# Two edits late in a two-block transformer kernel: where the second half of the odd attention's output is split, and where a norm's scale column is made

## The reference, cut to what matters

```python
def second_block(x, c, ctx, c_ctx, mod_w, mod_b, ...):
    for l in range(DEPTH):
        sh_a, sc_a, g_a, sh_f, sc_f, g_f = [m[:, None, :] for m in adaln(c, mod_w[l], mod_b[l])]
        ...
        hx = modulate(rms_norm_2(x, norm_mix_g[l]), sh_a, sc_a)
        ...
            y_x, y_c = odd_mixer(hx, hc, need_ctx, od_w_in[e], na_q_g[e], na_k_g[e], na_rpb[e])
        x = x + g_a * (y_x @ w_out[l])
        x = x + g_f * swiglu(modulate(rms_norm_2(x, norm_ffn_g[l]), sh_f, sc_f), ffn_w_in[l], ffn_w_out[l])
```

## Time and profile before

| | us |
|---|---|
| median of three runs | 2492.61 (2489.43 to 2493.49) |
| span of the profiled execution | 2492.5 |
| TensorE busy | 2455.0 (98%) |
| VectorE busy | 1663.2 (67%) |
| ScalarE busy | 1284.4 (52%) |
| GpSimd busy | 225.6 (9%) |

### The profile page before, as it was taken

One profiled execution on the slowest core, in us unless ns is written; L12 is line 12 of the kernel. 1 busy time (PEld: TensorE's weight loads), 2 busy tenths in 40 slices (PEclk: granted clock), 3 DMA queues, 4 the chain that ended last, 5 costly groups with the idle time before them and its releaser, 6 DMA issues.

```text
span 2492.5 us, 40595 instructions
## 1 busy us (share of the span) xinstructions
PE 2455.0 (98%) x16401; PEld 2145.3 (86%) x16401; DVE 1663.2 (67%) x2448; ACT 1284.4 (52%) x1858; POOL 225.6 (9%) x306
## 2 busy tenths in 40 slices
PE   8999999999999999999999999999999999999999
PEld 8998977889989988877898988888899898766998
DVE  5556786775566566776776668786666656776555
ACT  4444645444444446454564555655555445565443
POOL 1000000111002000000111201210000101211000
PEclk9999999999999999999999999999999999999999
DMA  8755565858658655556766546663456667735654
GB/s 285 243 181 179 145 189 158 287 176 299 199 177 275 189 159 165 173 167 227 234 218 183 187 137 212 193 209 120 133 177 197 190 183 203 219 120 177 195 186 144
DMA packets 239370, 479.14 MB, mean 192 GB/s; under 512 B 17584, under 2 KB 38328, under 8 KB 239120
## 3 DMA queue, kind: packets, MB, share of 16 engines
q1 hardware_dynamic: 215664, 397.07, 50.8%
q0 software_dynamic: 23520, 79.49, 9.9%
HBM read 475.33 MB, written 6.92 MB: 193 GB/s over the span
## 4 chain that ended last, share of the span: by engine, by line
PE 87%; DVE 6%; ACT 3%; DMA 2%; issue 2%; POOL 0%; ACTq 0%; SPq 0%; DVEq 0%; POOLq 0%
PE bank L213 84%; PE bank L216 3%; DVE wlo L156 1%; ACT whi L200 1%; DMA raw<-in_od_w_in 1%; DVE bank L161 1%; DVE xl L156 1%; DMA tbias<-t_rows 0%; ACT bank L200 0%; DMA raw<-in_w_mix_out 0%; ACT sps L200 0%; ACT po L200 0%; ACT lb L200 0%; DVE st L176 0%; POOL rs L148 0%
## 5 line engine op out<-in xcount | busy, mean ns | idle before, releaser
L156 DVE TENSOR_TENSOR wlo<-raw,whi 128x1024 fp32r<-128x1024 f32 (+3 forms) x786 | 914.8, 1171 | 616.4 <-ACT whi L200 614.8
L200 ACT ACTIVATE whi<-raw 128x1024 fp32r<-128x1024 f32 (+3 forms) x786 | 794.1, 1018 | 700.4 <-PE bank L213 646.7
L213 PE MATMUL bank<-xh,whi 128*128 128x256 f32 x2208 | 626.1, 284 | 4.2 <-DVE xl L156 3.1
L213 PE MATMUL bank<-xl,whi 128*128 128x256 f32 x2208 | 620.7, 281 | 0.0
L213 PE MATMUL bank<-xh,wlo 128*128 128x256 f32 x2208 | 620.7, 281 | 0.0
L213 PEld LDWEIGHTS bank<-xh,whi 128*128 128x128 f32 x2208 | 417.2, 189 | 15.7 <-issue 7.9
L213 PEld LDWEIGHTS bank<-xl,whi 128*128 128x128 f32 x2208 | 417.3, 189 | 0.6
L213 PEld LDWEIGHTS bank<-xh,wlo 128*128 128x128 f32 x2208 | 417.3, 189 | 0.0
L213 PE MATMUL bank<-whi,xh 128*128 128x512 f32 (+2 forms) x632 | 253.1, 401 | 8.3 <-DVE xl L156 3.9
L213 PE MATMUL bank<-wlo,xh 128*128 128x512 f32 (+2 forms) x632 | 245.6, 389 | 0.0
L213 PE MATMUL bank<-whi,xl 128*128 128x512 f32 (+2 forms) x632 | 245.5, 388 | 0.0
(11 more groups left out here) (455 smaller groups left out, 3763.0 us busy)
## 6 DMA issues: line engine op xcount, KB each, us to landing
raw<-in_ffn_w_in SPq DMA_DIRECT2D x280, 512.0 KB, 4.5
raw<-in_ffn_w_out SPq DMA_DIRECT2D x154, 512.0 KB, 4.5
raw<-in_w_mix_in SPq DMA_DIRECT2D x112, 512.0 KB, 3.6
store<-in_mod_w POOLq DMA_DIRECT2D x46, 512.0 KB, 7.8
raw<-in_od_w_in SPq DMA_DIRECT2D x40, 512.0 KB, 4.9
raw<-in_ffn_w_in SPq DMA_DIRECT2D x56, 256.0 KB, 2.8
stow<-in_mod_w POOLq DMA_DIRECT2D x28, 512.0 KB, 4.7
raw<-in_w_branch SPq DMA_DIRECT2D x24, 512.0 KB, 4.0
```

Source lines behind the costliest of these rows:

```text
L156: return self.passed(out, self.e and self.e.tensor_tensor(out, a, b, op))
L200: return self.made(us, self.e and self.e.activation(out, a, f, **k))
L213: return self.made(n, self.e and self.e.matmul(out, lhs, rhs, **k))
```

## The change

Two edits. In `prenorm`, the scale column is taken before the norm waits for the powers, if `co.modulated` already has what it needs; else at the old place. In `rows`, the attention job is wrapped in `attended`, which after the attention's last step splits the second half itself, into the same tiles `co.xt.hi` and `co.xt.lo`, with the same four operations that `halves` had; `second_half` is a new record of these tiles with marks of its own. The call of `halves` for the second half is gone, and the projection reads `second_half`.

```diff
@@ prenorm
         a[t] = co.po.tensor_tensor(st.rs[:, t, 1:2], st.rs[:, t, 0:1], minus_half(co, st.rs[:, t, 0:1]), ALU.pow).then_inc(co.s_po)
+    gain = mod_gain(co, l, f) if co.modulated >= for_norm(l, f) else None
     yield Need(a)
...
-    yield from modulated(co, for_norm(l, f))
-    gain = mod_gain(co, l, f)
+    if gain is None:
+        yield from modulated(co, for_norm(l, f))
+        gain = mod_gain(co, l, f)
@@ rows
-    heads = spawn(co, od.attend(co.Y, pr, at_, co.smo, co.mxo, at(92, "osel", [8, 512]), co.pn.tile[:, 512:1024], counts(co), done))
+    second_half = Turned(co.xt.hi, co.xt.lo)
+
+    def attended():
+        yield from od.attend(co.Y, pr, at_, co.smo, co.mxo, at(92, "osel", [8, 512]), co.pn.tile[:, 512:1024], counts(co), done)
+        y, second_half.dep = co.Y.tile[:, :, :].rearrange("p t d -> p (t d)").rearrange("p (k n) -> p k n", k=8), []
+        for k in (4, 6):
+            co.ac.wait_ge(tuple(done[1]), second_half.free)
+            a = co.ac.activation(second_half.hi[:, k:k + 2, :], y[:, k:k + 2, :], ACT.Copy).then_inc(co.s_ac)
+            co.dv.wait_ge(a)
+            second_half.dep.append(co.dv.tensor_tensor(second_half.lo[:, k:k + 2, :], y[:, k:k + 2, :], second_half.hi[:, k:k + 2, :].bitcast(F32), ALU.subtract).then_inc(co.s_dv))
+
+    heads = spawn(co, attended())
...
-    free = pe_mark(co)
+    free = second_half.free = pe_mark(co)
...
     while not heads.over:
         yield 0
-    co.xt.free = free
-    yield from halves(co, co.Y, 4, 8, tuple(done[1]), co.xt)
-    yield from out_proj(co, 1, 4, 8, co.xt, gate.make, True)
+    co.Y.free = second_half.dep[1]
+    yield from out_proj(co, 1, 4, 8, second_half, gate.make, True)
+    co.xt.free = pe_mark(co)
```

## The result

The changed kernel takes 2505.81 us (median; 2503.21 to 2507.33) where the kernel before takes 2492.61: a ratio of 1.0052, with a 95% interval of 1.0040 to 1.0063. It is 13 us slower, outside the range that was given, and not the 1.6 us faster that was forecast. Its profiled execution has a span of 2502.4 us, and the run that it belongs to is timed at 2504.39. TensorE does the same work: 2457.6 us busy with as many instructions as in the earlier trace rows.

The account below looks back on a forecast made before the run. TensorE was taken as the bound, busy 2455.0 of 2492.5 us. Terms -3.81 (A), +1.15 (B) and +1.2 (two feed-forward tiles) sum to -1.46, taken as -1.5: 2491.0 us, chance 0.52; range 2487.5 to 2496.0.

Parts of the forecast that it names:

- the term for the six earlier norms: At the six norms before the last, taking the scale early was put at 0, bounds 0 to -0.5 us.
- Rival 2: A readiness test on modelled times flips and rearranges jobs: 3.4 us either way, 2487.6 to 2494.4; chance 0.20.
- B: Around the last norm, up to the feed-forward's first product: TensorE 1.15 us later in the old clock.
- A: Start of the second output projection: its second half starts at 2276.08, not 2279.89, 3.81 us earlier.
- The two tiles pushed on from A: Two modulation tiles of the last but one block aren't done at A but in the last norm's first wait.
- the columns behind the multiplications at the last norm: At the last norm, `mc` follows the multiplications and the scale keeps its old place; ScalarE 0.2 us later from this.
- four loads ahead of the powers: At B, GpSimd issues four loads, not two, before the powers for the norm's roots, making them 0.7 us later.
- The two tiles in the feed-forward: Two modulation tiles stay over and go in the feed-forward's stream, costing 1.2 us.
- Rival 1: Last norm's block is ready, so the scale is taken during the powers: -2.95 us in all, 2489.5; chance 0.12.
- Rival 3: TensorE waits at the last norm and feed-forward for tiles not landed: +2.7 us, 2495.2; chance 0.12.
- Rival 4: The split isn't earlier in effect and the tiles stay at A: 2492.5 us; chance 0.04.
- The row against the early scale: A scale operation took 0.48 us beside GpSimd's ten loads, 0.17 elsewhere; each moved scale might cost up to 0.3 more.

Follow-up runs that it names:

- experiment 2: Kernel before with only the scale column made earlier, the split left in its old place: 2504.40 us, 1.0049.
- experiment 3: Kernel before with the scale column early in the engines' queues only, the plan modelling it at the old place: 2490.44 us, 0.9995.
- experiment 7: Whole change on the engines, but the plan given only the split, with the scale column modelled at its old place: 2490.76 us, 0.9989 of before.
- experiment 4: Kernel before with the scale column early in the plan only, the engines keeping it in the old place: 2503.26 us, 1.0043.
- experiment 5: Kernel before with one plan answer, no. 79 (are the first norm's multiplications ready), forced from yes to no: 2503.84 us, 1.0042.
- experiment 1: The change without its lines in prenorm, so the split alone: 2488.64 us against 2492.44 of before, 0.9986.
- experiment 8: Kernel before with the readiness test's spare constant 0.32 us instead of 0.30, nothing else: 2506.78 us, 1.0051.
- experiment 9: Split alone with the order's constants moved (spare 0.27, room 2.9, share 1.1), chosen for an early plan end: 2495.90 us, 1.0008 of before.

## Why the prediction was wrong

**The step that failed** is the term for the six earlier norms, which was put at 0: "The other six norms take the scale early, since their blocks are long done. The two operations are 0.17 each and go beside the powers on GpSimd ... so 0." The early scale measured +12.0 us (experiment 2). On the chip the 0 is right (experiments 3 and 7). In the plan it isn't: 10.8 us come with the plan's copy of the edit alone (experiment 4), and 10.7 with one answer (experiment 5). VectorE's modelled queue is behind at the first norm and not waiting for the powers, so what is put ahead of the multiplications makes them 0.43 us later. I counted what the scale no longer delays (a `wlo`) and not what it now stands in front of, and looked for the effect on TensorE's idle time only, not on the questions.

**Rival 2 named the mechanism** (a test that falls the other way) and was mis-sized. It was bounded by half the idle time of one late stretch, 3.4 us, and given 0.20. But a flip at 1290 has the rest of the kernel before it. In the profiled execution of the change, which is 9.9 us longer than that of before (6.6 of them from the last sum on), the stretch from 1500 to 1700 has 6.0 us more idle time, B is 8.19 us longer, four tiles more go into the feed-forward (2.40 us), and the split gives back 3.98 us at A. An order that was balanced can lose far more than the idle time it has; the idle time bounds only a gain. And "TensorE's times, to which they compare, are set by its own work" speaks for no flip only if the other side of the question doesn't move either. The margins, 0.398 for the answer 79 and less than 0.43 for three more of the same kind, could have been read from the plan before a range was set.

**The split's own terms**, from the split alone (experiments 1 and 7, the order of before upstream):
- A, -3.81: measured 15.88 against 19.78, -3.90. Right.
- The two tiles pushed on from A, the columns behind the multiplications at the last norm, four loads ahead of the powers: all as told. B, +1.15: measured +0.49. The loads follow one another at once, so the powers are 0.28 us later and not the 0.7 that I took from between the two patterns; and the four tiles behind the transposes take 2.05 us, not 2.5, so that they don't set the end. `xl` does, by the side that the sum had at +0.9: 0.28 from the powers and 0.20 for `mc`.
- The two tiles in the feed-forward, +1.2: measured +0.73 and +0.92.
- Sum -1.46: measured -2.7 by these stretches, -3.8 (0.9986) and -2.4 (0.9989) by the medians.

**The same split in the changed order is a loss**, by the stretches. There the tiles that lay under A's wait are part of eight on which the norm depends, and taking the wait at A away leaves B to pay. Scale only has 19.70 + 11.77 + 193.38 = 224.85 us from the sum to the end, the whole change 15.80 + 18.70 + 193.45 = 227.95: 3.1 us more, where the split gained 2.7 in the old order (221.34 to 218.66). By the medians it is 1.2, within the intervals.

**Rival 1** (scale early at the last norm): experiment 3 has this, since without the split the eleventh block is done at A. B is 1.15 us shorter; I had 0.68. By the medians it isn't to be told from no change. **Rival 3** (tiles not landed) did happen, for another reason than I gave: where up to four tiles were missing (experiments 1, 2, 4, 5, 7 and 8), none ahead of `modr` waited; with five the fifth waits 3.4 us, with eight TensorE waits 6.4 in all. Whether it waits is decided by the number of slots, how long by the landing. **Rival 4** is excluded by A.

**The row against the early scale** The earlier trace rows was read the wrong way round. The first scale operation at layer 1's first norm takes 0.48 us in all seven kernels that have it in the old place, where GpSimd issues its ten loads, and 0.16 to 0.17 in the five that have it early. VectorE and GpSimd of experiment 3:

```profile
2101.16 0.17 DVE L160 TENSOR_SCALAR mgain<-mc 128x16 f32<-128x16 f32 x1
```

```profile
2103.05 8.58 POOL L145 DMA_DIRECT2D nb<-rpb_rows  x10
```

These loads stand behind the powers in GpSimd's queue, so the early scale is done before them. Beside the powers it took 0.18 in experiment 3 and 0.16 at the first norm of after. So the 0.3 us that I allowed for was a cost of the old place, and no run shows it in the new one. The 0.48 agrees with the rule of the Trainium skill ("Advanced Engine Details and Errata", Mode Summary) on the port that VectorE shares with GpSimd; no run here tells the port from another cause, and the rule makes no difference to the kernel's time that these runs show.

The prediction also took the span of the profiled execution for the time of its run. The recorded runs are timed 1.8 to 2.1 us above the span of their core (after: 2504.39 and 2502.4). The forecast was a difference, so this changes nothing in it.

**What stays open.** Experiments 2, 4 and 5 lie 12.0, 10.8 and 10.7 us above the kernel before with orders that are the same (2 and 4) or nearly so; the differences are less than their intervals. Of the 13 us, the stretches are known, but the change in each is one of many that the flipped answer sets off, and they weren't undone singly. In experiment 5 only 1.2 us of the 10.7 lie behind the last sum, so most of the cost of that answer is upstream, and the waits near 1535 are the part of it that is shown. What each of the answers 383, 415 and 715 costs on the chip wasn't measured.

## What to carry to other kernels

Where an order is made from modelled times and thresholds, an edit on any engine is also an edit of the plan: compare the two orders instruction by instruction first, and where they part, ask for the margin of the question there. Give the plan and the engines the edit separately, as in experiments 3 and 4; it took two runs here to tell a dear instruction from a dear order. And before a wait is taken away, ask what had been put under it: filler on which nothing depends soon can be pushed on, filler that a later step needs comes back as a wait, as soon as it is more than the buffers hold.

## What the runs showed of the hardware

Loads from GpSimd's queue cost it 0.53 us each to issue, and the first 512 KB at B in experiment 9 were in use 4.4 us after the issue. With several in flight the median was longer. After, at B (operation, size, median us to landing):

```profile
stow<-in_mod_w POOLq DMA_DIRECT2D x6, 512.0 KB, 6.9
raw<-in_mod_w POOLq DMA_DIRECT2D x3, 512.0 KB, 5.6
```

A wait can cost TensorE more than its length. After the 4.42 us before `yc`, the 16 transposes took 3.68 us, at a granted clock of 0.50 (1.2 GHz). Before, the same 16 took 1.91 us with no wait ahead of them, in a stretch with a granted clock of 1.00 (2.4 GHz).

A 128x16 operation of VectorE took 0.48 us beside GpSimd's issue of ten loads in seven kernels, and 0.16 to 0.17 us ahead of them in five.
